# Summing the second norm's squares in pairs on VectorE, with three up tiles advanced in step, in a two-layer streaming encoder

## What is computed

```
h   = rmsnorm(x)                      # one combined projection, two attention branches, gates
mix = (sigmoid(ga) * y_a + sigmoid(gb) * y_b) @ w_out
x   = x + rmsnorm(mix, g_post_mix)    # "first norm" of this document: nm 1
u   = rmsnorm(x, g_pre_ffn) @ w_up    # "second norm": nm 2; u has 2 x 22 tiles of 128 features
uc  = conv_b + sum_i u_ext[:, i:i+T] * conv_w[i]
x   = x + rmsnorm((gelu(gate) * val) @ w_down, g_post_ffn)      # nm 3
x   = x + sigmoid(x @ w_ple_gate) * (p[i] @ w_ple_proj)         # tiles pleg, plep
```

## Time and profile before

| | before |
|---|---|
| median of 3 runs | 1819.49 us |
| the profiled execution, whole | 1819.9 us |
| its span, first to last instruction | 1818.1 us |
| TensorE matmul busy | 1803.8 us (99%) |
| VectorE busy | 1122.9 us (62%) |
| ScalarE busy | 664.0 us (37%) |
| GpSimd busy | 1186.7 us (65%) |

### The profile page before, as it was taken

One profiled execution on the slowest core, in us unless ns is written; L12 is line 12 of the kernel. 1 busy time (PEld: TensorE's weight loads), 2 busy tenths in 40 slices (PEclk: granted clock), 3 DMA queues, 4 the chain that ended last, 5 costly groups with the idle time before them and its releaser, 6 DMA issues.

```text
span 1818.1 us, 34666 instructions
## 1 busy us (share of the span) xinstructions
PE 1803.8 (99%) x14022; PEld 1745.1 (96%) x14022; DVE 1122.9 (62%) x1948; ACT 664.0 (37%) x1433; POOL 1186.7 (65%) x1396
## 2 busy tenths in 40 slices
PE   9999999999999999999999999999999999999999
PEld 8998989999999999999999988899999999999999
DVE  6666775332779579554656767752336795795554
ACT  4444553112535235323334444531134352352221
POOL 8676634656575875967676864346466758759584
PEclk9999999999999999999999999999999999999999
DMA  5242211324222222323342421122332222223222
GB/s 186 95 129 77 70 42 59 106 90 151 69 89 94 93 87 89 100 69 101 107 142 93 137 77 59 60 70 84 132 102 78 86 94 94 89 86 103 74 94 96
DMA packets 76239, 170.54 MB, mean 94 GB/s; under 512 B 6384, under 2 KB 34160, under 8 KB 76080
## 3 DMA queue, kind: packets, MB, share of 16 engines
q1 hardware_dynamic: 68752, 160.79, 27.3%
q10 hardware_dynamic: 7328, 7.54, 1.3%
HBM read 156.41 MB, written 9.79 MB: 91 GB/s over the span
## 4 chain that ended last, share of the span: by engine, by line
PE 93%; DVE 5%; ACT 1%; issue 1%; DMA 0%; POOL 0%; SPq 0%; DVEq 0%; ACTq 0%; POOLq 0%
PE ps L1927 63%; PE ps L2358 7%; PE ps L1980 4%; PE ps L2390 3%; PE ps L2108 3%; PE ps L2066 2%; PE ps L2019 1%; PE ps L2325 1%; DVE R L1328 1%; PE ps L2162 1%; PE ps L2168 1%; PE ps L1967 1%; PE ps L2085 1%; PE ps L2034 1%; PE ps L2104 1%
## 5 line engine op out<-in xcount | busy, mean ns | idle before, releaser
L1927 PE MATMUL ps<-xn,wsp 128*128 128x272 f32 x7824 | 1002.2, 289 | 2.9 <-DVE xn L1303 0.9
L1927 PEld LDWEIGHTS ps<-xn,wsp 128*128 128x128 f32 x7824 | 986.2, 189 | 7.9 <-issue 3.3
L749 POOL TENSOR_TENSOR wsp<-raw,wsp 128x256 fp32r<-128x256 f32 x656 | 505.8, 792 | 26.3
L744 POOL CAST wsp<-raw 128x512 fp32r<-128x512 f32 x328 | 229.6, 700 | 261.0 <-DMA raw<-in_wstream 199.3
L762 POOL TENSOR_TENSOR wsp<-raw,wsp 128x256 fp32r<-128x256 f32 (+1 forms) x174 | 209.2, 1224 | 6.6
L755 POOL CAST wsp<-raw 128x1024 fp32r<-128x1024 f32 (+2 forms) x102 | 94.4, 937 | 178.4 <-DMA raw<-in_wstream 160.8
L1927 PE MATMUL ps<-R,wsp 128*128 128x272 f32 x1632 | 209.4, 289 | 0.1
L1927 PEld LDWEIGHTS ps<-R,wsp 128*128 128x128 f32 x1632 | 205.9, 189 | 1.6 <-DVE xT L1357 0.5
L1328 DVE SCALAR_TENSOR_TENSOR R<-ps,R 128x512 fp32r<-128x512 f32 (+13 forms) x272 | 129.4, 499 | 66.1 <-ACT R L843 20.2
L737 POOL TENSOR_TENSOR wsp<-raw,wsp 128x512 fp32r<-128x512 f32 x64 | 95.0, 1504 | 66.5 <-DVE raw L1769 33.3
L1703 DVE SCALAR_TENSOR_TENSOR ps<-mix,vv,ps 128x546 f32<-128x546 f32 x88 | 69.5, 790 | 69.4 <-ACT ps L1163 69.4
(11 more groups left out here) (273 smaller groups left out, 2301.6 us busy)
## 6 DMA issues: line engine op xcount, KB each, us to landing
raw<-in_wstream SPq DMA_DIRECT2D x233, 512.0 KB, 3.5
raw<-in_wstream SPq DMA_DIRECT2D x48, 128.0 KB, 2.7
raw<-in_wstream SPq DMA_DIRECT2D x16, 384.0 KB, 3.0
raw<-in_kc SPq DMA_DIRECT2D x8, 512.0 KB, 3.7
raw<-in_vc SPq DMA_DIRECT2D x8, 512.0 KB, 4.3
xT<-in_x_in SPq DMA_DIRECT2D x8, 272.0 KB, 5.8
out_k_out<-mix ACTq DMA_DIRECT2D x8, 272.0 KB, 3.5
xT<-in_x_in SPq DMA_DIRECT2D x1, 2176.0 KB, 9.2
```

Of the source, the lines that this page charges most:

```text
L744: nc.gpsimd.tensor_copy(dst[:, 0, f], part[:, f]).then_inc(S["w_hi"], 1)
L749: ins = nc.gpsimd.tensor_tensor(dst[:, 1, f], part[:, f], dst[:, 0, f].bitcast(F32), ALU.subtract)
L1927: mm = pe.matmul(z[:, h], w[:, x, (k0 + k) * P:(k0 + k + 1) * P], rhs[:, y, k, h * HT:(h + 1) * HT], start=(k == 0 and (x, y) == (0, 0)), ...
```

## The change

Squares: VectorE adds the squares of two neighbouring tiles into `acc` (`add_pair`), in the residual loop behind the low part of an odd tile, and TensorE multiplies `acc` by the ones once for each pair: four times per layer in place of eight. ScalarE's next two squares wait for the addition, and the addition of the next pair waits until TensorE has read the last.

Tiles in step: `upg 1` joins `upg 0` and `upv 0` in `together`; its separate product and its wait on the residual's multiplications are gone. POOL's extra wait moves from `upg 1` (seven tiles of `x` updated) to `upv 1` (all eight). VectorE evacuates `upv 1` earlier, before the product of tile 0.

Factor: ScalarE writes the first norm's factor to `rstd` in SBUF instead of in place in PSUM, and the first residual's multiplications (L1676) read it there.

```diff
-        for t in FFN[0:2]:
+        for t in FFN[0:3]:
             EVENTS.append(("open", t))
-        for t in FFN[0:2]:
+        for t in FFN[0:3]:
             EVENTS.append(("done", t))
         whole(("nm", 2))
...
+        def pairs_added(layer, p):
+            return KT - 3 + KT // 2 * layer + p + 1
...
-                        if ch == ("upg", 1):
-                            pool.wait_ge(S["x_add"], KT - 1)
+                        if ch == ("upv", 1):
+                            pool.wait_ge(S["x_add"], KT)
...
-                            r = ptile(t)[:, h]
+                            z = ptile(t)[:, h]
+                            r = z if norm else rstd[:, h * HT:(h + 1) * HT]
                             act.wait_ge(S["p_done"], AT[part] + 1)
-                            ac(r, r, ACT.Ln, bias=epsb[:], scale=1.0 / D).then_inc(S["act_read"], 1)
+                            ac(r, z, ACT.Ln, bias=epsb[:], scale=1.0 / D).then_inc(S["act_read"], 1)
...
                         if j >= 2:
-                            act.wait_ge(S["sq2_sum"], j - 1)
+                            act.wait_ge(pre["added"], pairs_added(layer, j // 2 - 1))
                         ac(sq[j % 2], xT[:, j], ACT.Square).then_inc(S["sq2_done"], 1)
...
+                        def add_pair(p):
+                            dve.wait_ge(S["sq2_done"], 2 * p + 2)
+                            if p > 0:
+                                dve.wait_ge(S["sq2_sum"], p)
+                            v.tensor_tensor(acc[:], sq[0], sq[1], ALU.add).then_inc(pre["added"], 1)
...
                             v.scalar_tensor_tensor(halves(tmp[j % 2]), halves(fT[:, j]), vv[:, gain + j:gain + j + 1],
-                                                   ptile(("nm", which - 1)), ALU.mult, ALU.mult).then_inc(S["r_mul"], 1)
+                                                   halves(rstd[:]) if which == 2 else ptile(("nm", which - 1)),
+                                                   ALU.mult, ALU.mult).then_inc(S["r_mul"], 1)
...
                             if j > 0:
                                 low(j - 1)
+                            if which == 2 and j >= 2 and j % 2 == 0:
+                                add_pair(j // 2 - 1)
                         low(KT - 1)
+                        if which == 2:
+                            add_pair(KT // 2 - 1)
...
-                                u_tile(("upv", j))
+                                if j != 1:
+                                    u_tile(("upv", j))
...
                             taps(("upv", j))
+                            if j == 0:
+                                u_tile(("upv", 1))
                             product(j)
...
-                    def square_sum(j):
+                    def square_sum(k):
+                        if k % 2 == 0:
+                            return
                         z = ptile(("nm", 2))
-                        pe.wait_ge(S["sq2_done"], j + 1)
+                        pe.wait_ge(pre["added"], pairs_added(layer, k // 2))
                         for h in range(2):
-                            mm = pe.matmul(z[:, h], ones, sq[j % 2][:, h * HT:(h + 1) * HT], start=(j == 0), stop=(j == KT - 1),
+                            mm = pe.matmul(z[:, h], ones, acc[:, h * HT:(h + 1) * HT], start=(k == 1), stop=(k == KT - 1),
                                            skip_group_check=True)
...
-                    together(FFN[0:2], KT, square_sum)
+                    together(FFN[0:3], KT, square_sum)
...
-                        for t in [(n, j) for j in _run(i) for n in ("upg", "upv")][2 if i == 0 else 0:]:
-                            if t == ("upg", 1):
-                                pe.wait_ge(S["r_mul"], KT)
+                        for t in [(n, j) for j in _run(i) for n in ("upg", "upv")][3 if i == 0 else 0:]:
                             project(t, t, xn, KT)
```

More of the change, by code:

```diff
@@ L392, in build @@
         for i in range(len(FFN_PARTS)):
-            whole(*[(n, j) for j in _run(i) for n in ("upg", "upv")][2 if i == 0 else 0:])
+            whole(*[(n, j) for j in _run(i) for n in ("upg", "upv")][3 if i == 0 else 0:])
             if i == LAST:
@@ L2319, in _ @@
                         project(("plep", j), ("pp", j // 4), p_s, PLE // P, PLE // P * (j % 4))
-                    def square_sum(j):
+                    def square_sum(k):
+                        if k % 2 == 0:
+                            return
                         z = ptile(("nm", 2))
-                        pe.wait_ge(S["sq2_done"], j + 1)
+                        pe.wait_ge(pre["added"], pairs_added(layer, k // 2))
                         for h in range(2):
-                            mm = pe.matmul(z[:, h], ones, sq[j % 2][:, h * HT:(h + 1) * HT], start=(j == 0), stop=(j == KT - 1),
+                            mm = pe.matmul(z[:, h], ones, acc[:, h * HT:(h + 1) * HT], start=(k == 1), stop=(k == KT - 1),
                                            skip_group_check=True)
-                        mm.then_inc(S["sq2_sum" if j < KT - 1 else "p_done"], 1)
-                    together(FFN[0:2], KT, square_sum)
+                        mm.then_inc(S["sq2_sum" if k < KT - 1 else "p_done"], 1)
+                    together(FFN[0:3], KT, square_sum)
                     def down_product(n, i, j, ks=None):
```

## The result

The changed kernel takes 1822.2 us (median of 20 runs, 1820.64 to 1824.07) against 1819.5 us (20 runs); the ratio is 1.0014, 95% interval 1.0008 to 1.0021. It is slower by 2.7 us where 0.5 us was forecast: inside the range and inside 0.2%, but not by the sum of the prediction alone. The profiled execution is one of the shorter ones (1821.05 us, span 1819.2).

What follows compares the result with a forecast made beforehand. TensorE, busy 99% of the span, was taken as the bound. Per layer -3.68 (squares) + 2.74 (bare tail) + 1.2 (GpSimd collision) = +0.26 us, +0.5 in two layers: 1820.0 us, range 1816.8 to 1823.7.

Steps and rivals of the forecast that it cites:

- The squares: Square sums on TensorE: four of eight go, 3.68 us saved per layer, VectorE's pair additions costed at nothing.
- The bare tail: Behind the last square sum: `upv 1` waits for the evacuation of `upg 0`, no longer hidden under `upg 1`; 2.74 us per layer.
- The meeting with GpSimd: First residual: GpSimd's split of `upg 1` runs beside VectorE's first instructions and delays TensorE's first steps; 1.2 us per layer.
- the rule on the shared port: First residual's multiplications, both operands in SBUF, are blocked beside a split: 1.26 us, not 0.77; otherwise 0.4 us less per layer.
- The reserve before `upg 3`: Feed-forward: VectorE evacuates `upg 2` in 17.6 us against TensorE's 18.0; 0.4 us reserve, costed at nothing, 0.7 at the upper end.
- third rival: TensorE's bare tail brings its clock down, some 1.9 us each time, 3.8 in two layers: 1824 us; chance 8%.
- fourth rival: VectorE does not catch up, feed-forward reserve used up, GpSimd collision at its upper end: +2.1 us per layer, 1823.7; chance 8%.

Runs made afterwards that it cites:

- the run that covers it: Changed kernel with the last four k-tiles of `upg 1` (24 matmuls) moved behind the last square sum; 1815.1 us against 1819.8, ratio 0.9976.
- The thin split: Changed kernel with GpSimd's split of `upg 1` cut to a sixteenth of its columns and `upg 1` multiplied with the high part alone; 1818.2 us.
- the repetition: The changed kernel run again, unchanged, on the chip of three other runs; 1821.9 us, ratio 1.0015.
- work in the gap: Changed kernel with six, or three, extra unread products behind the last square sum in each layer; 1821.1 us with six, 1820.7 us with three.

## Why the prediction held its range and missed its number

**The squares: right.** A sum is 0.92 us, four are saved per layer, and TensorE never waits for a pair. The run without pairs is 2.9 us longer in the passage, as four sums less the wait of the second step that they cover. The prediction did not ask what the pairs do without the third tile; alone they are worth nothing.

**The bare tail: right.** Forecast 2.74 us, measured 2.79. That it is the main loss is shown by the run that covers it: 2.45 us per layer and all the falls came back.

**The meeting with GpSimd: right in kind, too small.** Forecast 1.2 us: 0.9 for the first step and 0.3 for the second. By starts, the first step comes 7.06 us behind `plep` instead of 6.21, 0.85; the second, 3.06 behind the first instead of 2.25, 0.8. In sum 1.65. The second part was undersized: the last subtractions ran to 462.13, so the third multiplication and the third addition were slowed whole (1.25 and 1.15). The rows of before had it: in the second residual 3.10 us lie between the end of the first low part, 863.37, and the second step, 866.47; here they are 3.11 (460.35 to 463.46). A small part of the 0.85 is not the meeting: the residual starts 1.77 us behind `plep` instead of 1.63, as it also does in the run with the factor alone, because ScalarE's four instructions on `rstd` take longer (0.43 for an exponential instead of 0.38). The thin split took 1.46 of it away. The weighing of the rule on the shared port (the Trainium skill, SBUF — State Buffer, "Who interferes with whom") came out for the rule: the multiplication, which stood at 0.77 beside a split while its factor was in PSUM, takes 1.26 with both operands in SBUF; the run with the factor alone, where nothing else was changed, shows the same at the first cast (0.77 and 1.13).

**The reserve before `upg 3`: right by a hair.** Forecast 17.6 us against 18.0. In layer 1, where the clock stayed, the evacuation of `upg 2` ended at 1407.30, 18.2 us behind that of `upg 0` at 1389.13, and TensorE needed 18.1 for its three tiles: no wait of note shows, and no reserve. The estimate was 0.6 us too short. Putting the evacuation back made 0.8 us of waits.

```profile
1388.95 0.18 DVE L1713 TENSOR_TENSOR mix<-ps,rstd 128x32 f32<-128x32 f32 x1
...
1407.13 0.17 DVE L1713 TENSOR_TENSOR mix<-ps,rstd 128x32 f32<-128x32 f32 x1
```

**The sum without the clock.** -3.68 + 2.79 + 1.65 = +0.8 us per layer, +1.5 in two. The runs without a fall are three: two here, 1.2 above 1819.5, and one of the repetition, 0.3 above the 1819.1 of its chip. Those with work in the gap stand 1.0 and 1.3 above their before. Forecast +0.5.

**The clock: the step that failed.** The prediction took its fall as a rival with 8%, because the clock row of the page before never falls and no wait is longer than 1.5 us. The row was no evidence: the 1.7 us that a fall loses leave a slice of 45 us at 0.96, a nine. Taken by the microsecond (columns as above), the trace of before does hold a fall, at its end. TensorE's last matmul ends at 1814.58, and some 2.6 us later the granted clock goes down:

```profile
1814.00:1815.00 1.00, 0.58 (x5) 0.36 (x3) 0.00 (x0) 0.38 (x1) 0.00 (x0) 1.00 0.23 82
1815.00:1816.00 1.00, 0.00 (x0) 0.00 (x0) 0.89 (x2) 0.00 (x1) 0.00 (x0) 1.00 0.00 0
1816.00:1817.00 1.00, 0.00 (x0) 0.00 (x0) 0.00 (x0) 0.00 (x0) 0.00 (x0) 1.00 0.15 55
1817.00:1818.00 1.00, 0.00 (x0) 0.00 (x0) 0.00 (x0) 0.00 (x0) 0.00 (x0) 0.61 0.24 84
```

The sum put the fall at nothing without looking there. The third rival's mechanism came true in two of three gaps, at 1.4 us each instead of 1.9. The 1.9 us per run are most of the miss. They should have stood in the sum as a term with a price and a chance, not beside it: a gap longer than any in the trace was the one thing that the change was certain to make. That the time still lies inside the range is luck: the upper end, 1823.7, was made of the fourth rival's collision and reserve, of which only a part came, and the third rival had been left out of it; single runs with two falls go up to 1824.07.

Where 1.7 us of clock shrink to 1.5 us on the first tile was not traced. How much of those 1.5 us reaches the end depends on VectorE: 1.44 after three tiles in the changed kernel, 0.65 with the evacuation put back, where TensorE would have waited for it anyway.

## What to carry to other kernels

A saving on the busiest engine is worth what the next engine's pace allows: the pairs alone gained nothing, since VectorE's loop had become the bound. When work is pulled into a loop, ask what it covered where it stood; part of it can be left there (24 of 48 matmuls were enough). And when a change opens a gap on TensorE that is longer than any in the trace before, put the fall of its clock into the sum; look for falls in stretches of a microsecond, at the end of the kernel too, since a row of 40 slices hides them.

## What the runs showed of the hardware that was not expected

TensorE's granted clock fell to 0.50 in 41 of 62 cases behind a gap of 2.8 us (a bare wait of 2.4 us), and in none of 22 behind one whose bare wait was 1.2 us, nor in the 22 with a wait of 1.28 us (pairs alone). In three other kernels with the wait of 2.4 us it fell in 6 of 8, 10 of 22 and 13 of 22 cases. In the trace of the changed kernel the fall came while TensorE was at work again, 0.4 us or more behind the restart (1.00 in the stretch to 486, 0.67 in the next), and cost 1.4 us. It can also come before: with three tiles and no pairs, where TensorE starts again at 488.44, the clock is down already at 488.10 (columns as for the first tile above).

```profile
488.10:488.40 0.30, 0.00 (x0) 0.50 0.79 287
```
